# Transposed rows by token halves, and the first gate tile projected half by half

## The reference

```python
x = x + mixer(rmsnorm(x, norm_mix[i]), ...)
x = x + conv_ffn(rmsnorm(x, norm_ffn[i]), w_up, conv_w, conv_b, w_down)   # first model, both layers
x = x + swiglu(rmsnorm(x, norm2[0]), gate, up, down)                      # second model, layer 0
x = x + moe_swiglu(rmsnorm(x, norm2[1]), router, gate, up, down)          # second model, layer 1
```

## Time and profile before

| what | value |
|---|---|
| median of three runs | 1714.12 us |
| profiled execution | 1716.91 us, its span 1715.1 us |
| PE busy | 1624.3 us |
| DVE busy | 1163.1 us |
| ACT busy | 963.2 us |
| mean granted clock of PE | 0.978 |

### The profile page before, as it was taken

One profiled execution on the slowest core, in us unless ns is written; L12 is line 12 of the kernel. 1 busy time (PEld: TensorE's weight loads), 2 busy tenths in 40 slices (PEclk: granted clock), 3 DMA queues, 4 the chain that ended last, 5 costly groups with the idle time before them and its releaser, 6 DMA issues.

```text
span 1715.1 us, 30039 instructions
## 1 busy us (share of the span) xinstructions
PE 1624.3 (95%) x11794; PEld 1443.0 (84%) x11794; DVE 1163.1 (68%) x1346; ACT 963.2 (56%) x1256; POOL 25.7 (2%) x37
## 2 busy tenths in 40 slices
PE   5977999999989999999999999999889999999997
PEld 5966999989978999899889998998678888888885
DVE  4455776664457676686765445777549988988885
ACT  4554545555546455573453444734447777777773
POOL 0000000000000000020000000200000000000000
PEclk9988999999999999999999999999989999999998
DMA  6532455534414555362155554531329999999993
GB/s 236 186 108 95 163 184 196 175 144 166 155 73 162 185 193 186 134 203 101 51 192 178 193 188 156 179 121 54 148 82 378 350 349 360 361 359 347 350 353 114
DMA packets 48225, 339.15 MB, mean 198 GB/s; under 512 B 5776, under 2 KB 5952, under 8 KB 8192
## 3 DMA queue, kind: packets, MB, share of 16 engines
q1 hardware_dynamic: 46064, 330.94, 52.5%
q0 software_dynamic: 2064, 6.83, 1.3%
HBM read 336.66 MB, written 1.10 MB: 197 GB/s over the span
## 4 chain that ended last, share of the span: by engine, by line
PE 51%; DVE 3%; ACT 3%; issue 1%; ACTq 0%; DVEq 0%
PE PS L1553 15%; PE PS L857 8%; PE PS L1571 8%; PE PS L1624 7%; PE PS L1641 4%; PE PS L1209 2%; PE PS L1508 1%; PE PS L1583 1%; DVE ARENA L2753 1%; PE PS L1536 1%; DVE MWL L2415 1%; PE PS L934 1%; ACT MWH L1781 0%; PE PS L1523 0%; ACT HN L1717 0%
## 5 line engine op out<-in xcount | busy, mean ns | idle before, releaser
L2957 DVE TENSOR_TENSOR EWL<-W,EWH 128x2048 fp32r<-128x2048 f32 x144 | 329.0, 2290 | 45.3 <-ACT EWH L2210 45.2
L2210 ACT ACTIVATE EWH<-W 128x2048 fp32r<-128x2048 f32 x144 | 276.2, 1919 | 67.7 <-PE PS L1571 36.7
L1624 PE MATMUL PS<-HTH,WH 128*128 128x256 f32 x1056 | 299.1, 283 | 5.3 <-DVE HTL L2387 5.3
L1624 PE MATMUL PS<-HTL,WH 128*128 128x256 f32 x1056 | 298.7, 283 | 0.0
L1624 PE MATMUL PS<-HTH,WL 128*128 128x256 f32 x1056 | 298.6, 283 | 0.0
L2410 DVE TENSOR_TENSOR WL<-W,WH 128x2048 fp32r<-128x2048 f32 x99 | 226.3, 2288 | 103.1 <-ACT WH L1763 102.1
L2415 DVE TENSOR_TENSOR MWL<-W,MWH 128x1024 fp32r<-128x1024 f32 x138 | 169.8, 1237 | 148.5 <-ACT MWH L1781 140.7
L1781 ACT ACTIVATE MWH<-W 128x1024 fp32r<-128x1024 f32 x138 | 144.3, 1055 | 190.8 <-PE PS L857 182.6
L1763 ACT ACTIVATE WH<-W 128x2048 fp32r<-128x2048 f32 x99 | 189.3, 1915 | 60.2 <-PE PS L1624 32.7
L1624 PEld LDWEIGHTS PS<-HTH,WH 128*128 128x128 f32 x1056 | 201.1, 190 | 7.0 <-issue 5.9
L1624 PEld LDWEIGHTS PS<-HTL,WH 128*128 128x128 f32 x1056 | 201.2, 191 | 1.1
(11 more groups left out here) (326 smaller groups left out, 2814.9 us busy)
## 6 DMA issues: line engine op xcount, KB each, us to landing
W<-in_weights SPq DMA_DIRECT2D x312, 1024.0 KB, 4.8
ARENA<-rows_m POOLq DMA_DIRECT2D x8, 192.0 KB, 5.7
ARENA<-rows_m POOLq DMA_DIRECT2D x2, 768.0 KB, 10.3
CS<-in_consts POOLq DMA_DIRECT2D x3, 403.0 KB, 5.3
X<-in_x SPq DMA_DIRECT2D x2, 512.0 KB, 3.7
out<-X SPq DMA_DIRECT2D x1, 1024.0 KB, 4.2
PR<-in_params SPq DMA_DIRECT2D x1, 830.0 KB, 7.8
CS<-in_consts POOLq DMA_DIRECT2D x2, 403.5 KB, 5.2
```

The costliest lines, as they stand in the source:

```text
L1624: ins = mm(PS[b][:, c * 256:(c + 1) * 256], wt[:, sl, o:o + P], ht[:, kk, :], start=(kk == 0 and n == 0), stop=(kk == KC - 1 and n == 2))
L2210: A(EWH[tile % SPLIT][:, :], tile_ap(w0 + tile), ACT.Copy).then_inc(sem("moe_hi"), 1)
L2957: TT(EWL[tile % SPLIT][:, :], tile_ap(w0 + tile), EWH[tile % SPLIT][:, :].bitcast(F32), SUB).then_inc(sem("moe_lo"), 1)
```

## The change

The transposed rows of norms 1, 3 and 5 are made in halves of 128 tokens. `turn_tokens(n, t)` transposes one half's eight chunks into two banks, PS6 and PS7 for half 0, PS0 and PS1 for half 1; chunk c lies in bank c % 2. ACT and DVE make HTH and HTL chunk by chunk for half 0 and then for half 1, in pieces of 128x128. ACT's Silu table load stands behind all sixteen copies. PE projects the first gate tile with products of 128 tokens: half 0 column block 0, then the transposes of half 1, half 0 block 1, half 1 block 0, half 1 block 1. Counters of the other norms are renumbered (left out below); everything else is as before.

```diff
+    FFN_NORMS = (1, 3, 5)
     def plan_norm(n):
         for b in range(4):
-            plan(("norm", n, b), 4 + b)
+            plan(("norm", n, b), (6, 7, 0, 1)[b] if n in FFN_NORMS else 4 + b)
...
+        def turn_tokens(n, t):
+            for b in (2 * t, 2 * t + 1):
+                claim(pe, ("norm", n, b))
+            for c in range(KC):
+                if c % 4 == 0:
+                    pe.wait_ge(sem("hn"), 2 * (NT * n + t) + c // 4 + 1)
+                key = ("norm", n, 2 * t + c % 2)
+                ins = pe.transpose(bank(key)[:, c // 2 * P:(c // 2 + 1) * P], HN[:, t, c * P:(c + 1) * P], ident)
+                if c >= KC - 2:
+                    done(ins, key)
         def norm(n):
+            if n in FFN_NORMS:
+                return turn_tokens(n, 0)
...
+            def gate_by_tokens(n, b, sl):
+                for t in range(NT):
+                    for c in range(2):
+                        if t == 0 and c == 1:
+                            turn_tokens(n, 1)
+                        for kk in range(KC):
+                            if c == 0:
+                                pe.wait_ge(sem("ht_part"), 16 * FFN_NORMS.index(n) + 8 * t + kk + 1)
+                            o = kk * TW + c * P
+                            for m, (wt, ht) in enumerate(((WH, HTH), (WH, HTL), (WL, HTH))):
+                                ins = mm(PS[b][:, c * 256 + t * P:c * 256 + (t + 1) * P], wt[:, sl, o:o + P], ht[:, kk, t * P:(t + 1) * P],
+                                         start=(kk == 0 and m == 0), stop=(kk == KC - 1 and m == 2))
+                return ins
...
-                    for c in range(2):
+                    if first and half == 0:
+                        ins = gate_by_tokens({"ffn0": 1, "ffn1": 3, "ffn2": 5}[name], b, sl)
+                    for c in range(0 if first and half == 0 else 2):
                         for kk in range(KC):
-                            if first and half == 0 and c == 0:
-                                await_chunk({"ffn0": 1, "ffn1": 3, "ffn2": 5}[name], kk)
...   ACT, norm(n)
-            if n in ffn_of_norm:
-                act.preload_act_table(ACT.Silu)
+            if n in FFN_NORMS:
+                for t in range(NT):
+                    for c in range(KC):
+                        key = ("norm", n, 2 * t + c % 2)
+                        if c < 2:
+                            await_full(act, key)
+                        else:
+                            act.wait_ge(sem("ht_part"), 16 * FFN_NORMS.index(n) + 8 * t + c - 1)
+                        A(HTH[:, c, t * P:(t + 1) * P], bank(key)[:, c // 2 * P:(c // 2 + 1) * P], ACT.Copy,
+                          scale=g[:, n * KC + c:n * KC + c + 1]).then_inc(sem("ht_part_hi"), 1)
+                act.preload_act_table(ACT.Silu)
+                for k in range(EARLY, SPLIT):
+                    hi(ffn_of_norm[n], k, 0)
+                return
...   DVE, norm(n)
+            if n in FFN_NORMS:
+                for t in range(NT):
+                    for c in range(KC):
+                        key = ("norm", n, 2 * t + c % 2)
+                        dve.wait_ge(sem("ht_part_hi"), 16 * FFN_NORMS.index(n) + 8 * t + c + 1)
+                        ins = STT(HTL[:, c, t * P:(t + 1) * P], bank(key)[:, c // 2 * P:(c // 2 + 1) * P], g[:, n * KC + c:n * KC + c + 1],
+                                  HTH[:, c, t * P:(t + 1) * P].bitcast(F32), MUL, SUB)
+                        ins.then_inc(sem("ht_part"), 1)
+                        if c >= KC - 2:
+                            dve.wait_ge(sem("ht_part"), 16 * FFN_NORMS.index(n) + 8 * t + c + 1)
+                            dve.sem_inc(free[uses[key][0]], 1)
+                for k in range(1, SPLIT):
+                    lo(ffn_of_norm[n], k, 0)
+                return
```

More of the change, by code:

```diff
@@ L880, in await_chunk @@
             if k == 0:
-                pe.wait_ge(sem("ht_lo"), 4 * n + b + 1)
+                pe.wait_ge(sem("ht_lo"), 4 * (n - sum(f < n for f in FFN_NORMS)) + b + 1)
             else:
@@ L1735, in norm @@
                     else:
-                        act.wait_ge(sem("ht_lo"), 4 * n + b + 1)
+                        act.wait_ge(sem("ht_lo"), 4 * (n - sum(f < n for f in FFN_NORMS)) + b + 1)
                     if n == 0 and c == 4:
@@ L1742, in norm @@
                     feed(n)(SPLIT - 1)
-                if n in ffn_of_norm:
-                    for k in range(EARLY, SPLIT):
-                        hi(ffn_of_norm[n], k, 0)
                 return
@@ L2385, in norm @@
                         feed(n)(1)
-                    dve.wait_ge(sem("ht_hi"), 8 * n + c + 1)
+                    dve.wait_ge(sem("ht_hi"), 8 * (n - sum(f < n for f in FFN_NORMS)) + c + 1)
                     ins = STT(HTL[:, c, :], bank(("norm", n, b))[:, k * 256:(k + 1) * 256], g[:, n * KC + c:n * KC + c + 1],
@@ L2392, in norm @@
                         release(ins, ("norm", n, b))
[L2393 to L2397, removed]
+                feed(n)(SPLIT - 1)
                 return
```

## The result

| | before | after |
|---|---|---|
| median, us | 1715.03 (4 runs, 1714.1 to 1716.54) | 1755.88 (4 runs, 1749.9 to 1761.06) |
| profiled execution, span | 1715.1 | 1757.0 |
| mean granted clock of PE | 0.978 | 0.96 |

The ratio is 1.0239, with a 95% interval of 1.0218 to 1.026: 41 us slower, where 10.7 us were forecast and 1731 us was the end of the range.

What follows compares the result with a forecast made beforehand. PE was taken to bound each feed-forward stage from first to last product. Three stages 8.5 us longer plus 2.2 for the clock gave 10.7 us, 1724.8 us from 1714.1; range 1718 to 1731.

Steps and rivals of the forecast that it cites:

- The clock: Gate tiles of three stages: a fall to half clock costs 1.5 us each, 0 to 4.5 together; 2.2 taken.
- the sum: Three feed-forward stages, first transpose to value tile: 8.5 us longer, plus 2.2 for the clock, 10.7 in all.
- The first product: Start of the gate tile: first product 2.40 us after the first transpose, 2.08 us earlier than before.
- The narrow product at full clock: Gate tile: a 128-column product costs 0.112 to 0.118 us, 0.115 taken.
- Pacing, transposes, remainders: Gate tile: 0.2 us for pacing in block 0, 0.9 for half 1's transposes; value tile 14.55 us after first transpose.
- a floor under the narrow product: Gate tile: a 128-column product falls on the price of its weight reload, about 0.11 us at full clock.
- The cover for the remainders: Value tile: its weight remainder is there at 183.9, 2.4 us before it is wanted at 186.31.
- The plain f32 run of the earlier trace: Trace before: read as 18 products of 128x128 in plain f32 at full clock, 0.112 us each.
- The 32 products of 8 columns: Trace before: read as 0.22 us each at half clock, so 0.11 at full clock, the price of the reload.
- (b): Rival, gate tiles: the clock falls in every stage, perhaps twice, 8.5 + 4.5 to 8.5 + 9, 1727 to 1732; 15 in 100.
- (c): Rival, gate tile: narrow products run at a quarter of the rate, 0.213 us, 12.1 us a stage, 1750.5; 6 in 100.
- (a): Rival, gate tile: the weight reload is hidden, 0.081 us a product, 1.0 us in all, 1715.1; 13 in 100.

Runs made afterwards that it cites:

- e9: The changed kernel with 11 spare wide products a stage in PE's two gaps ahead of the first gate tile; 1728.4 us, ratio 1.0069 to the kernel before.
- e2: The kernel before with only the first gate tile of each feed-forward stage in 96 products of 128 columns; 1761.4 us, ratio 1.0262.
- e1: The changed kernel with the same narrow products in plain f32 instead of fp32r; 1759.8 us, ratio 1.0262 to the kernel before.
- e11: The kernel before with both up tiles of group 1 in narrow products, 192 without a pause between wide ones; 1747.8 us, ratio 1.0175.
- e12: The kernel of e2 with 16 spare wide products after the first 24 narrow ones; 1747.0 us, ratio 1.0179 to the kernel before.

## Why the prediction was wrong

**The step that failed is "The clock".** It priced a fall of the clock at "the 1.5 us of now, 16 x (0.213 - 0.118)", that is, it took from the kernel before not only that the clock falls but also how soon it is back. In the rows before, it came back while wide products ran; the change takes those away for the whole tile. In the first stage 81 narrow products ran at the lower clock, 81 x (0.213 - 0.112) = 8.2 us, the transposes between them cost 0.7 more and the value tile 2.3: 11.2 us where I had 1.5 at the most. Against e9, whose clock is at 1.00, the end of the value tile's starts comes 11.0, 12.4 and 9.5 us later in the three stages (31.10, 32.54 and 29.66 for 20.12, 20.11 and 20.12): 33 us for the clock, where the sum had 2.2 (the two spans differ by 31.0). e2 shows that the narrow products alone do this, e9 that without the low clock it is gone.

**The rest of the sum held.** The first product: 2.36 us for 2.40. The narrow product at full clock: 0.112 us, in my bracket of 0.112 to 0.118, 0.115 taken. Pacing, transposes, remainders: value tile after 14.40 us (e9) for 14.55. Up to the end of the value tile's starts the three stages of e9 are 8.2 us longer than before (20.12, 20.11 and 20.12 for 17.34, 17.43 and 17.42), for 8.5 in the sum without the clock term, and these 8.2 with the 33 of the clock make up the 41; the whole kernel is 0.69% slower, 11.8 us by the ratio (8.6 to 15.1). So the forecast's mechanism, a floor under the narrow product, is right, and only its term for the clock is not. The cover for the remainders held too: no value product waited for WL.

**Two rows were misread.** The plain f32 run of the earlier trace rows is not 18 products but 9, two matmuls each, as e1 shows; the count in the code, 36 products for 72 in the group, would have told me. The 32 products of 8 columns are 16, for the same reason. They gave the right floor only because each matmul of the pair reloads its weights (18 weight loads to 18 matmuls in the earlier trace rows). And the earlier trace rows had the answer in view: 8-column products with PE busy for 2.00 of 2.00 us and the clock still at 0.50. I read the price of a reload there and not the clock. An earlier run of such products (L1481, from 1228.53, behind 1.74 us without work) shows the fall as well, at 1230.7, with PE busy for the 2.2 us before it:

```profile
1229.40:1230.40 1.00, 1.00 (x11) 1.00 (x11) 1.00 1.02 426
1230.40:1231.40 1.00, 1.00 (x8) 1.00 (x8) 0.67 1.02 434
1231.40:1232.40 1.00, 1.00 (x6) 1.00 (x6) 0.50 0.56 221
```

**The rivals.** (b) had the right kind of loss, a fall of the clock in every stage, and at its most (9 us) about a quarter of its size (33): it let the clock fall more than once, where in fact it fell once and stayed. The pacing of block 0, which it blames too, is still there in e9, and the clock doesn't fall. (c) came nearest in time, 1750.5, for the wrong reason: the product does cost 0.213, but at half clock, and 0.112 at full. (a) is refuted by the 0.112 of e9; the 81 ns that the Trainium skill gives (TensorE: Matmul & The Clock Gate, Back-to-back issue gap) isn't reached by this type.

**What stays open.** Why plain f32 products of the same width and spacing brought the clock back, or kept it up (e1), and fp32r ones didn't, was not tried further; that each of the two matmuls of a plain f32 product takes 0.22 us for 256 columns at full clock (L1154 of the kernel before), where an fp32r one takes 0.118, and so streams each column longer, fits, but is argued and not shown. Nor is it shown why four executions of the kernel after spread over 11 us; the first four of the kernel before spread over 2.4, but 23 others over 8.5. Falls of the clock that come at other points in each would do that.

## What to carry to other kernels

When a change makes matmuls narrower, ask not only what one costs but whether such products lift a clock that has fallen ahead of them: where a stage begins behind a gap, begin it with wide products, or fill the gap with spare ones, and measure. Look in the old trace for any dense run of products of the new width and type and read its granted clock, not only its pace. And try the small parts of a change by themselves: here the bank and the table load were worth 0.2% that the large part buried.

## What the hardware showed that I had not expected

- Narrow fp32r products (128 columns over 128x128 weights) start 0.112 us apart at the upper clock and 0.213 at the lower, so half the columns save 0.006 us of 0.118, and nothing at the lower clock.
- Where no gap lies ahead of them they keep either level: 0.50 for over 16 us in e2 with PE always busy, 1.00 for the 21.3 us of e11. In e12 it changed while 16 wide ones ran.
- A plain f32 product is two matmuls in the trace, 0.224 us for 128 columns, twice the fp32r one, and products of this type, though as narrow, brought the clock back in 3.4 us (second stage of e1).
